# The triangular inverse of a chunked RWKV scan: transposes removed, the inverse and its transpose updated by two sets of products side by side

## What is computed

```
def step(state, inp):
    r_t, w_t, k_t, v_t, a_t, b_t = inp
    sa = jnp.einsum('bhvk,bhk->bhv', state, a_t)
    state = (state * w_t[:, :, None, :]
             + sa[..., None] * b_t[:, :, None, :]
             + v_t[..., None] * k_t[:, :, None, :])
    y_t = jnp.einsum('bhvk,bhk->bhv', state, r_t)
    return state, y_t
```

## Time and profile before

| | |
|---|---|
| time, median of 3 runs (lowest to highest) | 1465.37 us (1463.49 to 1465.62) |
| profiled execution: its time, its span | 1464.72 us, 1462.9 us |
| PE busy, MATMUL records | 96% of the span, 10582 |
| DVE busy, ACT busy | 61%, 49% |
| the scan in the span | about 787 to 905 us, 8% |

### The profile page before, as it was taken

How to read it: one execution, slowest core, us unless ns; L and a number is a source line. 1 busy time by engine, 2 the same in 40 slices (tenths; PEclk the granted TensorE clock), 3 DMA queues, 4 the chain that set the end, 5 groups by cost and what they waited for, 6 DMA issues and landing times.

```text
span 1462.9 us, 25741 instructions
## 1 busy us (share of the span) xinstructions
PE 1401.1 (96%) x10582; PEld 1180.9 (81%) x10582; DVE 891.1 (61%) x1230; ACT 721.5 (49%) x987; POOL 140.7 (10%) x141
## 2 busy tenths in 40 slices
PE   8989999999999999999999988999999988899998
PEld 8956988987997998885676777799998765699997
DVE  5566655557476555565976677565456666455563
ACT  5454654445545544445564343454354655354452
POOL 0162011100000101100100102000000223000000
PEclk9999999999999999999999999999999999999999
DMA  8733565565646566554553000556474631265472
GB/s 297 233 109 101 189 207 175 170 189 173 204 142 214 168 218 189 187 173 165 172 145 115 4 3 19 169 166 198 156 240 141 215 99 58 64 222 180 145 234 76
DMA packets 86429, 231.29 MB, mean 158 GB/s; under 512 B 15860, under 2 KB 21636, under 8 KB 86312
## 3 DMA queue, kind: packets, MB, share of 16 engines
q1 hardware_dynamic: 85752, 227.53, 48.7%
q0 software_dynamic: 560, 2.11, 0.4%
HBM read 228.53 MB, written 1.08 MB: 157 GB/s over the span
## 4 chain that ended last, share of the span: by engine, by line
PE 84%; DVE 8%; ACT 3%; issue 2%; POOL 2%; DMA 1%; SPq 0%; DVEq 0%; ACTq 0%; POOLq 0%
PE PS L430 50%; PE PS L433 31%; PE PS L445 3%; DVE SL L408 1%; POOL AB L807 1%; ACT SH L402 1%; DVE SL L405 1%; DVE AB L781 1%; POOL SM L875 0%; DMA ST<-in_w_attn_in 0%; DVE X L696 0%; ACT AB L791 0%; DVE LG L1671 0%; DVE MG L1680 0%; ACT XH L593 0%
## 5 line engine op out<-in xcount | busy, mean ns | idle before, releaser
L408 DVE SCALAR_TENSOR_TENSOR SL<-ST,SM,SH 128x1024 fp32r<-128x1024 f32 (+1 forms) x256 | 314.9, 1249 | 171.2 <-ACT SH L402 135.2
L402 ACT ACTIVATE SH<-ST,SM 128x1024 fp32r<-128x1024 f32 (+1 forms) x256 | 282.3, 1122 | 198.5 <-PE PS L433 118.6
L430 PE MATMUL PS<-XH,SH 128*128 128x256 f32 x1224 | 344.2, 281 | 1.2 <-DVE XL L594 1.2
L433 PE MATMUL PS<-XH,SL 128*128 128x256 f32 x1224 | 344.4, 281 | 0.0
L430 PE MATMUL PS<-XL,SH 128*128 128x256 f32 x1224 | 343.4, 281 | 0.0
L405 DVE TENSOR_TENSOR SL<-ST,SH 128x1024 fp32r<-128x1024 f32 (+1 forms) x153 | 196.0, 1296 | 154.9 <-ACT SH L402 130.7
L402 ACT ACTIVATE SH<-ST 128x1024 fp32r<-128x1024 f32 (+1 forms) x153 | 158.3, 1051 | 153.1 <-PE PS L433 130.9
L430 PEld LDWEIGHTS PS<-XH,SH 128*128 128x128 f32 x1224 | 231.3, 189 | 2.6 <-ACT SH L402 1.4
L430 PE MATMUL PS<-SH,XH 128*128 128x512 f32 x544 | 221.8, 408 | 11.7 <-DVE SM L796 2.6
L430 PEld LDWEIGHTS PS<-XL,SH 128*128 128x128 f32 x1224 | 229.0, 187 | 0.9
L433 PEld LDWEIGHTS PS<-XH,SL 128*128 128x128 f32 x1224 | 229.2, 187 | 0.2
(11 more groups left out here) (308 smaller groups left out, 1470.0 us busy)
## 6 DMA issues: line engine op xcount, KB each, us to landing
ST<-in_ffn_w_gu SPq DMA_DIRECT2D x80, 512.0 KB, 4.5
ST<-in_w_mlp_up SPq DMA_DIRECT2D x64, 512.0 KB, 4.7
ST<-in_w_mlp_down SPq DMA_DIRECT2D x64, 512.0 KB, 4.4
ST<-in_ffn_w_down SPq DMA_DIRECT2D x44, 512.0 KB, 4.3
ST<-in_w_attn_in SPq DMA_DIRECT2D x24, 512.0 KB, 4.5
ST<-in_w_conv_in SPq DMA_DIRECT2D x24, 512.0 KB, 4.6
ST<-in_w_ple_gate SPq DMA_DIRECT2D x16, 512.0 KB, 4.3
ST<-in_kv_w SPq DMA_DIRECT2D x16, 512.0 KB, 3.7
```

The source lines that it names most:

```text
L402: a = ac.do(lambda e: e.activation(h[p0:p1, 0:cols], t[p0:p1, 0:cols], ACT.Copy, scale=sc), ready, t_gt, pe_done.get(i - NSPLIT))
L408: b = ve.do(lambda e: e.scalar_tensor_tensor(l[p0:p1, 0:cols], t[p0:p1, 0:cols], sc, h[p0:p1, 0:cols].bitcast(F32), ALU.mult, ALU.subtract ...
L430: pe.go(lambda e: e.matmul(o, l, r, start=start, stop=stop, skip_group_check=skip))
L433: return pe.do(lambda e: e.matmul(o, l, r, start=start, stop=stop, skip_group_check=skip))
```

## The change

1. The masks of the levels (`C_LV`) get the identity added. Z is then "identity plus the masked product", where before it was the masked product alone.
2. So that the product gives the diagonal too, LG gets the identity added, with one more DVE operation a lane behind that of MG (L1681 of the changed kernel), so that L·X brings X's own diagonal.
3. XX and XT become two halves of one tile XB. Levels 0 to 3 make both new halves from Z: 8 products XT·Z and, side by side with them, 8 products Z·XT that give the transpose directly. One plain copy of 128x512 elements brings both to SBUF: on ACT (L1727), for pair 2 on DVE (L1725). The additions L1718 and the flips of the levels are gone. The flip in `head` stays.
4. The fifth level makes only the transpose, and of it only the right half (8 products with a moving operand of 32 columns, and a copy on ACT, L1730).
5. The order of the products alternates between levels, since the halves of the tile swap their roles of head and chunk.

```
-        c[:, C_LV + 64 * n:C_LV + 64 * (n + 1)] = ((r6 // m) % 2 == 1) & ((q6 // m) == (r6 // m) - 1)
+        c[:, C_LV + 64 * n:C_LV + 64 * (n + 1)] = (((r6 // m) % 2 == 1) & ((q6 // m) == (r6 // m) - 1)) | (r6 == q6)
...
         free_both(z, z.mg)
+        z.lg = ve.do(lambda e: e.tensor_tensor(LG[:, :, :, 0:64], LG[:, :, :, 0:64], m4(C_I64, 64), ALU.add), z.lg)
         yield
         flip(z)
...
         for n in range(5):
+            def bx(m, hl):
+                return (m, hl) if n % 2 else (hl, m)
+
+            tiles = [(c, m, hl) + bx(m, hl) for u1 in range(2) for c in range(2) for u0 in range(2) for m, hl in ([(u0, u1)] if n % 2 else [(u1, u0)])]
             wait_banks(z.bk)
             pe.wait(z.xx, z.lg)
-            t = products(z, [(ob(z, c, m * 64, 64, hl), LG[hf(c), hl, m, 0:64], XX[hf(c), m, hl, :]) for m, c, hl in quads])
+            t = products(z, [(ob(z, c, x * 64, 64, b), LG[hf(c), hl, m, 0:64], XB[hf(c), x, 0, b, :]) for c, m, hl, b, x in tiles])
...
-            t = products(z, [(ob(z, hl, m * 64, 64, c), XT[hf(hl), m, c, :], Z[hf(hl), c, m, :]) for m, c, hl in quads])
-            xp = XX[:, :, :, :].rearrange("p m b j -> p b m j")
-            z.xx = ve.do(lambda e, xp=xp: e.tensor_tensor(xp, xp, two(z, 0, 128).rearrange("p b (m j) -> p b m j", m=2), ALU.add), t)
-            free_both(z, z.xx)
-            yield
-            flip(z)
+            if n < 4:
+                t = products(z, [(ob(z, b, x * 64, 64, c), XB[hf(b), x, 1, c, :], Z[hf(b), c, x, :]) for c, m, hl, b, x in tiles]
+                             + [(ob(z, b, 128 + c * 64, 64, x), Z[hf(b), c, x, :], XB[hf(b), x, 1, c, :]) for c in range(2) for x in range(2) for b in range(2)])
+                dst = XB[:, :, :, :, :].rearrange("p b u x j -> p b (u x j)")
+                if p == 2:
+                    z.xx = z.xt = ve.do(lambda e, dst=dst: e.tensor_copy(dst, two(z, 0, 256)), t)
+                else:
+                    z.xx = z.xt = ac.do(lambda e, dst=dst: e.activation(dst, two(z, 0, 256), ACT.Copy), t)
+            else:
+                t = products(z, [(ob(z, m, c * 32, 32, hl), Z[hf(hl), c, m, :], XB[hf(hl), m, 1, c, 32:64]) for m in range(2) for c in range(2) for hl in range(2)])
+                z.xt = ac.do(lambda e: e.activation(XB[:, :, 1, :, 32:64], two(z, 0, 64).rearrange("p m (c i) -> p m c i", c=2), ACT.Copy), t)
+            free_both(z, z.xt)
             yield
```

More of the change, by code:

```diff
@@ L1608, in emit @@
         z.MG = cut("MG", 0, 6144, [128, 2, 2, 128])
-        z.XX = cut("XX", 1, 0, [128, 2, 2, 64])
-        z.XT = cut("XT", 1, 1024, [128, 2, 2, 64])
+        z.XB = cut("XB", 1, 0, [128, 2, 2, 2, 64])
         z.Z = cut("Z", 1, 2048, [128, 2, 2, 64])
@@ L1653, in head @@
         fr = z.fr
-        T4, LG, MG, XX, XT, AM = z.T4, z.LG, z.MG, z.XX, z.XT, z.AM
+        T4, LG, MG, AM = z.T4, z.LG, z.MG, z.AM
+        x_ = z.XB[:, :, 0, :, :]
         flat = T4[:, :, :, :].rearrange("p m x t -> p m (x t)")
@@ L1671, in head @@
         z.lg = ve.do(lambda e: e.tensor_tensor(LG[:, :, :, :], two(z, 0, 256).rearrange("p b (m t) -> p b m t", m=2), sx, ALU.mult), t, fr)
-        x0 = ve.do(lambda e: e.tensor_tensor(XX[:, :, :, :].rearrange("p m b j -> p b m j"),
-                                             two(z, 256, 128).rearrange("p b (m j) -> p b m j", m=2), m4(C_M1, 64), ALU.mult), t, z.tail_free)
+        x0 = ve.do(lambda e: e.tensor_tensor(x_.rearrange("p m b j -> p b m j"), two(z, 256, 128).rearrange("p b (m j) -> p b m j", m=2), m4(C_M1, 64), ALU.mult), t, z.tail_free)
         free_both(z, x0)
-        x0 = ve.do(lambda e: e.tensor_tensor(XX[:, :, :, :], XX[:, :, :, :], m4(C_I64, 64), ALU.add), x0)
+        x0 = ve.do(lambda e: e.tensor_tensor(x_, x_, m4(C_I64, 64), ALU.add), x0)
         z.xx = x0
@@ L1698, in flip @@
         for m in range(2):
-            t = tr_t(bank(b, m * 128, m * 128 + 128), z.XX[:, m, :, :].rearrange("p b j -> p (b j)"))
-        z.xt = ac.do(lambda e: e.activation(z.XT[:, :, :, :].rearrange("p m c i -> p (m c i)"), bank(b, 0, 256), ACT.Copy), t, z.tail_free)
+            t = tr_t(bank(b, m * 128, m * 128 + 128), z.XB[:, m, 0, :, :].rearrange("p b j -> p (b j)"))
+        z.xt = ac.do(lambda e: e.activation(z.XB[:, :, 1, :, :], bank(b, 0, 256).rearrange("p (m c i) -> p m c i", m=2, c=2), ACT.Copy), t, z.tail_free)
         bfree[b] = z.xt
     def solve(p, z):
-        LG, XX, XT, Z, AM, WZ = z.LG, z.XX, z.XT, z.Z, z.AM, z.WZ
+        LG, XB, Z, AM, WZ = z.LG, z.XB, z.Z, z.AM, z.WZ
         for n in range(5):
+            def bx(m, hl):
+                return (m, hl) if n % 2 else (hl, m)
+            tiles = [(c, m, hl) + bx(m, hl) for u1 in range(2) for c in range(2) for u0 in range(2) for m, hl in ([(u0, u1)] if n % 2 else [(u1, u0)])]
             wait_banks(z.bk)
             pe.wait(z.xx, z.lg)
-            t = products(z, [(ob(z, c, m * 64, 64, hl), LG[hf(c), hl, m, 0:64], XX[hf(c), m, hl, :]) for m, c, hl in quads])
-            zt = ve.do(lambda e, n=n: e.tensor_tensor(Z[:, :, :, :], two(z, 0, 128).rearrange("p c (m j) -> p c m j", m=2), m4(C_LV + 64 * n, 64), ALU.mult),
+            t = products(z, [(ob(z, c, x * 64, 64, b), LG[hf(c), hl, m, 0:64], XB[hf(c), x, 0, b, :]) for c, m, hl, b, x in tiles])
+            zt = ve.do(lambda e, n=n: e.tensor_tensor(Z[:, :, :, :], two(z, 0, 128).rearrange("p c (x j) -> p c x j", x=2), m4(C_LV + 64 * n, 64), ALU.mult),
                        t, z.tail_free)
@@ L1724, in solve @@
         pe.wait(z.xt, z.am)
-        t = products(z, [(ob(z, hl, m * 128, 128, c), XT[hf(hl), m, c, :], AM[hf(hl), c, m, :]) for m, c, hl in quads])
+        t = products(z, [(ob(z, hl, m * 128, 128, c), XB[hf(hl), m, 1, c, :], AM[hf(hl), c, m, :]) for m, c, hl in quads])
         z.wz = ac.do(lambda e: e.activation(WZ[:, :, :, :].rearrange("p b m x -> p b (m x)"), two(z, 0, 256), ACT.Copy), t, z.tail_free)
```

## The result

The changed kernel takes 1479.74 us (median of 6 runs, 1478.97 to 1484.72), the kernel before 1465.49 in the same comparison; the ratio is 1.0097, 95% interval 1.0079 to 1.0114. That is 14.2 us longer, where 12.0 were summed. The profiled execution has a span of 1477.4 us against 1462.9, 14.5 longer. The forecast was 1476.5 us, in a range of its own from 1472 to 1481.

What follows compares the result with a forecast made beforehand. The prediction took PE's instruction fetching, 3.69 us per 128 records, to bound most of the scan. First round 7.3 plus second 4.65 gave 12.0 us on 1464.72, or 1476.7, stated as 1476.5 us; own range 1472 to 1481, 8-in-10 range 1467 to 1482.

Steps and rivals of the forecast that it cites:

- What bounds the scan: Most of the scan: PE does 128 MATMUL records, then waits for its next instructions; mean interval 3.69 us.
- Records and blocks: Both rounds of the scan: 432 more PE records, 3.4 blocks of 128, gross price 12.5 us at 3.69 us each.
- the sign: Expected in the changed profile's scan: DVE idle before Z for more than 2 us a level.
- First round: First round of the scan: last block border 8.4 us later, fewer records behind it give back 1.1; 7.3 us longer.
- Second round: Second round of the scan: last border 3.3 us later, with 48 more records at 28 ns behind it; 4.65 us longer.
- The credit for levels 0 and 1: Second round: these levels waited for DVE; four additions a level go and fetching fills that time, so under half the gross price.
- The addition to LG: In `head`: four more DVE operations at 0.32 us between the MG operations; last lane's MG and PE 1.0 us later each round.
- Copies: Levels 0 to 3: copies take 0.52 us a lane on ACT, 2.06 us a level, and make nothing late.
- the chain decides: Faster rival: waits, not fetching, pace the scan; levels of 2.85 us, -13.6 us together, 1451 us; chance 0.09.
- PE's own time: Rival named with the experiments, no chance given: PE's time for added products sets the cost, 14.5 ns a record.
- The short interval: Rival of nearly no change: scan intervals of 3.29 us throughout, +2 to +4 us, 1467 us; chance 0.09.

Runs made afterwards that it cites:

- second trace of the kernel before: The kernel before, unchanged, executed and traced once more: one run of 1461.65 us, its scan 107.6 us against 110.1 in the first trace.
- twice the copies: The changed kernel with each copy of XB on ACT in levels 0 to 3 done twice: 1479.68 us, ratio 1.0114 to the kernel before.
- the last level alone: The kernel before with only a shortened fifth level: right half of the transpose, added on DVE, no flip; 1464.87 us, ratio 1.0005.
- the wide products: The kernel before with a moving operand of 128 instead of 64 columns in L·X, no record more: 1468.1 us, ratio 1.0022.
- L·X twice and three times: The kernel before with each level's products L·X issued two or three times into the same place: 1479.84 us, ratio 1.0121, and 1499.94 us, ratio 1.0246.
- the single set: The changed kernel with only the first of two product sets in levels 0 to 3, copied to both halves (output wrong): 1461.07 us, ratio 0.9987.

## Why the prediction came out as it did

The measured 1479.74 us lie 3.2 above the forecast and inside its range, and the mechanism was the one that the runs show. That the sum came so close is luck in part: the first round cost 2.3 us more than summed and the second 1.0 less, and the two executions differ by another 1.3 outside the scan.

*What bounds the scan* was read rightly from the gaps and the packets. Kernels with 10502, 10582, 11014, 11222 and 11862 records have ratios of 0.9987, 1, 1.0097, 1.0121 and 1.0246 to the kernel before, in that order, and those that change the copies, the chain or PE's time and leave the records (but for 16) move by 0.22% at the most from the kernel that they start from. The Trainium skill, "Advanced Engine Details and Errata", section "ISA Cache", gives the store of instructions two lines of 256 instructions; that agrees with one packet per 128 records and a wait at each border. The same section gives TensorE 128 KB, and the page that the prediction names says 2048 instructions; a store of that size is not seen in any run.

*Records and blocks.* 11014 records, 87 packets, 28 in the scan, as forecast; levels were 5.2 us in the first round (Z of level 0 at 806.49, of level 4 at 827.43, in four levels), just under the 5.3 to 5.8 given, and 5.45 in the second (870.25 to 892.06). The gaps of the levels were 0.7 to 1.9 us, wider apart than the 1.3 to 1.8 given; DVE was idle ahead of Z for 22.2 us in ten levels, 2.2 a level, as the sign asked.

*First round, +9.6 where the step gave +7.3.* The mechanism held, sizes were off. The first gap ends at 810.57, which less the 2.0 us ahead of the scan is 808.5; the step had its second border at 803.04 + 1.0 + 3.69 = 807.7. The 0.8 come from the stretch before:

```profile
800.00:808.00 8.00, 7.26 (x234) 6.29 (x237) 3.46 (x9) 3.54 (x7) 0.00 (x0) 0.57 0.01 2
```

PE's granted clock is 0.57 of 2.4 GHz there, that is, at 1.2 GHz for most of it, after PE had waited for DVE in `head`. A lane's products for AM take 0.74 us in the chain, where the first trace of the kernel before has 0.40:

```profile
803.43 0.74 PE PS L430 x27
...
804.29 0.74 PE PS L430 x27
```

So PE passed the first border, record 52 of `solve`, without a gap at 807.16, 1.1 us later than the step had it, and its next block took 3.41 us instead of 3.69. I had counted the products of AM at half pace only in the second round. The second trace of the kernel before has 0.57 there as well (798 to 802, where the first has 1.00), so the change need not be its cause. From there, nine intervals took 34.49 us instead of 9 x 3.69 = 33.2, another 1.3. Together 2.1 of the 2.3.

*Second round, +3.6 where the step gave +4.65.* The credit for levels 0 and 1, which had waited for DVE, came as argued. Most of the missing 1.0 us lies in one block. The chain has the ends of the first and the last gap of this round at 872.39 and 905.45:

```profile
871.61 0.78 issue
...
904.63 0.82 issue
```

The step put the border before them, in AM, 12.3 us behind LG and the next one 3.69 later, at 16.0; PE passed the first without a gap and had its next block 872.39 - 857.11 = 15.3 us behind LG, 0.75 earlier. The nine intervals from there took 33.06 us, 3.67 each, as priced. Where PE does not wait at a border, the next packet follows sooner: here 0.7 us behind it (869.26 to 869.94) instead of 1.1.

*The addition to LG* is 0.33 us each, as priced; its price in the whole time was not resolved. *Copies* were hidden, as priced, with less room than the text suggests.

*The rivals.* That the chain decides in the changed kernel is excluded by its own levels, of 5.2 us and more with gaps that nothing releases where the chain needs 2.85, and by the first round with twice the copies; that it decides alone in the kernel before, by the last level alone. PE's own time is excluded by the wide products, by L·X twice and three times and by the single set. The short interval did occur for single blocks (3.37 us at the least between two gaps of the changed kernel), but not as the rule: the means were 3.83 and 3.67 us.

## What to carry to other kernels

Count a rewrite in instructions of PE too, not only in its time. Here, where 128 records with their weight loads were done in 2.4 us, each further 128 cost 3.6 us, and widening as many of them cost a fifth of that; eight 64x64 products of float32 in place of two transposes are 16 records against 2. The sign in a profile is a gap with no releaser at each 128th record and one packet of the instruction queue per gap.

A shorter chain gave nothing behind such a border. Before taking steps out of a chain, look whether the chain or the border ends last; in this kernel they were level, so that removing waits could bring next to nothing and adding instructions cost their full price.

## What was not expected of the hardware

The interval of one and the same program differs between executions: blocks at 3.29 to 4.00 us in one trace of the kernel before, and levels at 3.47 us a block, on its edge, in the other.

The records of the queue's packets show what an interval is made of where a gap stands at both ends of a block. After PE has entered a block, the packet of the next one starts 1.0 to 1.7 us later and takes 0.9 to 1.5 us, and PE enters that next block 1.2 to 1.6 us after the packet's end. In the first trace of the kernel before, for example, the gap ends at 803.05, the packet runs from 804.17 for 1.47 us, and the next gap ends at 807.05; in the interval of 3.29 us from 825.97 the packet starts at 827.09 and takes 0.93. In the scan the next block is thus not fetched until PE has entered the one before it, and the three parts add up to the interval. The packets of the scan took 1.13 us in the mean in that trace and 0.97 in the second one. Why they are longer in one execution than in another no run here tells.

Doubling the columns of a product set (64 to 128) at the same instruction count cost 3 us over the whole kernel, doubling its instructions at the same columns 16 to 18 us.
